# One kernel for a mixer, a mixture of experts and two gated layers: the first h tiles made in pairs, other counts of fillers, fewer transpositions ahead of the last sums

## The reference, cut to what matters

```python
mod = silu(c) @ w_mod + b_mod                       # 6 x 1024
sh1, sc1, gt1, sh2, sc2, gt2 = split(mod, 6)
h = rms_norm(x, g_norm1) * (1.0 + sc1) + sh1        # the opening
mix = hybrid_mixer(h, w_in, ...)                    # proj = h @ w_in and what follows
x = x + gt1 * mix
...                                                 # experts, then the second block
x = x + rms_norm(ffn2(rms_norm(x, g_pre)), g_post) * 0.5   # the end
```

## Time and profile before

| | |
|---|---|
| median of 3 runs | 2126.43 us (2124.46 to 2127.33) |
| profiled execution | 2119.8 us, its span 2117.8 us |
| PE busy | 2043.9 us, 97% of the span |
| DVE, ACT, POOL busy | 61%, 40%, 38% |
| mean granted TensorE clock | 0.980 |
| chain that ended last | PE 88%, DVE 6%, ACT 3% |

### The profile page before, as it was taken

How to read it: one execution, slowest core, us unless ns; L and a number is a source line. 1 busy time by engine, 2 the same in 40 slices (tenths; PEclk the granted TensorE clock), 3 DMA queues, 4 the chain that set the end, 5 groups by cost and what they waited for, 6 DMA issues and landing times.

```text
span 2117.8 us, 31232 instructions
## 1 busy us (share of the span) xinstructions
PE 2043.9 (97%) x12460; PEld 1745.8 (82%) x12460; DVE 1283.7 (61%) x1948; ACT 840.9 (40%) x1028; POOL 798.8 (38%) x605
## 2 busy tenths in 40 slices
PE   4999999999989999999999999999999998999998
PEld 4698787888767666679999999888878788999997
DVE  7375476665565666678677676331431359777775
ACT  7441355222354455544333333343332234333334
POOL 1342233544400000036666562221244545756661
PEclk7998999999999999999999999999999999999999
DMA  9121222555416999912322221211223212333321
GB/s 272 40 81 59 84 78 91 174 193 179 138 61 218 337 343 343 328 60 100 100 97 90 102 90 58 63 58 60 60 80 100 80 60 80 100 100 111 105 100 60
DMA packets 175763, 261.16 MB, mean 123 GB/s; under 512 B 12233, under 2 KB 140922, under 8 KB 175662
## 3 DMA queue, kind: packets, MB, share of 16 engines
q1 hardware_dynamic: 174126, 257.65, 36.4%
q10 hardware_dynamic: 1536, 2.10, 0.3%
HBM read 257.62 MB, written 2.11 MB: 123 GB/s over the span
## 4 chain that ended last, share of the span: by engine, by line
PE 88%; DVE 6%; ACT 3%; issue 1%; DMA 1%; SPq 0%; DVEq 0%; ACTq 0%
PE PS L829 65%; PE PS L1387 7%; PE PS L1427 4%; PE PS L1573 1%; PE PS L923 1%; ACT mod_early L1778 1%; PE PS L937 1%; DVE Hf L2428 1%; PE PS L1360 1%; PE PS L1442 1%; PE PS L1525 1%; DMA mod_early<-in_w_mod 1%; PE PS L1068 0%; PE PS L1028 0%; DMA w_raw<-in_w_ffn_in 0%
## 5 line engine op out<-in xcount | busy, mean ns | idle before, releaser
L740 POOL TENSOR_TENSOR w_lo<-w_raw,w_hi 128x512 fp32r<-128x512 f32 x444 | 596.0, 1373 | 1229.8 <-ACT w_hi L1756 871.1
L829 PE MATMUL PS<-HH,w_hi 128*128 128x512 f32 (+2 forms) x1408 | 469.1, 344 | 18.6 <-DVE HL L2351 4.6
L829 PE MATMUL PS<-HL,w_hi 128*128 128x512 f32 (+2 forms) x1408 | 464.7, 341 | 0.0
L829 PE MATMUL PS<-HH,w_lo 128*128 128x512 f32 (+2 forms) x1408 | 463.3, 340 | 0.0
L1756 ACT ACTIVATE w_hi<-w_raw 128x2048 fp32r<-128x2048 f32 x133 | 254.7, 1915 | 350.4 <-DVE w_raw L2389 124.8
L829 PEld LDWEIGHTS PS<-HH,w_hi 128*128 128x128 f32 x1408 | 262.1, 191 | 57.0 <-issue 15.2
L829 PEld LDWEIGHTS PS<-HH,w_lo 128*128 128x128 f32 x1408 | 262.1, 191 | 30.3
L829 PEld LDWEIGHTS PS<-HL,w_hi 128*128 128x128 f32 x1408 | 261.7, 190 | 29.3
L749 POOL TENSOR_TENSOR wx_lo<-wx_raw,wx_hi 128x512 fp32r<-128x512 f32 x132 | 187.7, 1450 | 0.0
L2926 DVE TENSOR_TENSOR m_lo<-m_raw,m_hi 128x2048 fp32r<-128x2048 f32 x56 | 128.3, 2292 | 70.0 <-ACT m_hi L2072 69.7
L3186 DVE TENSOR_TENSOR yacc<-yacc,PS 128x528 f32<-128x528 f32 (+1 forms) x176 | 117.9, 691 | 46.1 <-PE PS L829 44.7
(11 more groups left out here) (499 smaller groups left out, 4061.8 us busy)
## 6 DMA issues: line engine op xcount, KB each, us to landing
w_raw<-in_w_in SPq DMA_DIRECT2D x49, 1024.0 KB, 5.0
w_raw<-in_w_ffn_in SPq DMA_DIRECT2D x44, 1024.0 KB, 4.9
m_raw<-in_w_exp_gate SPq DMA_DIRECT2D x56, 512.0 KB, 4.0
m_raw<-in_w_exp_up SPq DMA_DIRECT2D x56, 512.0 KB, 5.2
m_raw<-in_w_exp_down SPq DMA_DIRECT2D x56, 512.0 KB, 4.7
w_raw<-in_w_ffn_out SPq DMA_DIRECT2D x22, 1024.0 KB, 4.8
mod_late<-in_w_mod SPq DMA_DIRECT2D x16, 1024.0 KB, 5.2
mod_early<-in_w_mod SPq DMA_DIRECT2D x8, 1024.0 KB, 11.9
```

The lines of the kernel that those rows point to most:

```text
L740: ins = pool.tensor_tensor(w_lo[:, s, cs], w_raw[:, s, cs], w_hi[:, s, cs].bitcast(F32), ALU.subtract)
L829: ins = mm(o, l, r, **k)
```

## The change

It touches four places.

1. **Loads.** SP loads w_mod tiles 0, 4, 1, 5, then the first w_in chunk, then tiles 2, 6, 3, 7.
2. **Opening.** Tiles 1, 2, 4 and 5 are multiplied by c on PE, tile 0 on DVE as before, and only 6, 3 and 7 go by ACT and DVE. They are worked through in the order 4, 0, 1, 5, 2, 6, 3, 7: PE does the first five ahead of the first chunk, 6 and 3 ahead of its k = 4, and 7 ahead of its k = 5. Gain, h, HH and HL are made for one pair of k at a time, on ACT with the scaling of 6, 3 and 7 between pairs 1 and 2. The results lie in the second bank of the slots, outside of the claims. ACT copies the second chunk's high part behind that of the small weights instead of ahead of it.
3. **Fillers.** hold goes from 8 to 11 in the norm behind the first mixer and in the one behind the first FFN, and in the norm behind the last mixer from 8 to 15, its idle from 28 to 14.
4. **End.** Only k = 0 to 3 are transposed ahead of the sums, for all four t; k = 4 to 7 behind them. The wait for the last released slots ahead of k = 4 goes.

```diff
...
-        MOD_PE = (1,)
-        MOD_SEQ = (1, 0, 2, 3, 4, 5, 6, 7)
+        MOD_PE = (1, 2, 4, 5)
+        MOD_SUMS = (0, 6, 3, 7)
+        MOD_SEQ = (4, 0, 1, 5, 2, 6, 3, 7)
+        MOD_LOADS = (0, 4, 1, 5), (2, 6, 3, 7)
...
-            for n in range(MOD1):
+            for n in MOD_LOADS[0]:
                 load_mod(n)
             cols("w_in", P1[0])
+            for n in MOD_LOADS[1]:
+                load_mod(n)
...
+            def early_mod(n):
+                at_ = MOD_SEQ.index(n)
+                if at_ >= SLOTS:
+                    pe.wait_ge(gain_ready, (at_ - SLOTS) // 2 + 1)
+                for m in range(2):
+                    o = PS[:, at_ % SLOTS, 1, m:m + 1]
+                    if n in MOD_PE:
+                        raw, landed, count = mod_slot(n)
+                        if m == 0:
+                            pe.wait_ge(landed, count)
                         for k in range(KT):
+                            ins = mm(o, raw[:, k, P * m:P * m + P], c_act[:, k:k + 1], start=k == 0, stop=k == KT - 1)
+                    else:
+                        d = mod_dve(n)
+                        if m == 0:
+                            pe.wait_ge(macc_ready, d + 1)
+                        ins = mm(o, macc[:, d % 2, P * m:P * m + P], ones[:, 0:1], start=True, stop=True)
+                ins.then_inc(mod_made, 1)
...
-            for n in MOD_SEQ:
-                mod_tile(n)
+            for n in MOD_SEQ[:5]:
+                early_mod(n)
...
             for k in range(KT):
+                if k == 4:
+                    early_mod(6)
+                    early_mod(3)
+                if k == 5:
+                    early_mod(7)
                 pe.wait_ge(hl_ready, hcount["hl"] + k + 1)
...
-            norm(SEQ, SQ_DENSE, 8, 5)
+            norm(SEQ, SQ_DENSE, 11, 5)
...
-            norm(TALL, SQ_DENSE, 8, 28)
+            norm(TALL, SQ_DENSE, 11, 28)
...
-            norm(SEQ, SQ_DENSE, 8, 28)
+            norm(SEQ, SQ_DENSE, 15, 14)
...
-            for k in range(KT - 1):
+            for k in range(4):
                 pe.wait_ge(yg_ready, k + 1)
-                if k == 4:
-                    for m in range(4, KT):
-                        W.wait_released(downs_at + m)
-                for t in range(NTOK - 1 if k >= 4 else NTOK):
+                for t in range(NTOK):
                     rows_of_y((s + 1 + t) % SLOTS, t, k)
...
-                for k in range(KT - 1 if t < NTOK - 1 else 4, KT):
+                for k in range(4, KT):
                     ins = rows_of_y(slot, t, k)
...
+            first_h(0)
             next_hi()
+            first_h(1)
+            scale_mod(6)
+            scale_mod(3)
+            scale_mod(7)
+            first_h(2)
+            first_h(3)
...
+            L(first_scaled(0, 2))
+            early_evac(4)
+            early_evac(0)
+            first_gain(0)
+            W.release(first_scaled(2, KT))
             W.wait_released(W.g - 1)
+            first_lo(0)
+            early_evac(1)
+            early_evac(5)
+            first_gain(1)
+            first_lo(1)
+            early_evac(2)
+            mod_sum(6)
+            mod_sum(3)
+            early_evac(6)
+            first_gain(2)
+            mod_sum(7)
+            early_evac(3)
+            first_lo(2)
+            early_evac(7)
+            first_gain(3)
+            first_lo(3)
```

More of the change, by code:

```diff
@@ L405, in build @@
         merged_tile = sem("merged_tile_final")
+        mod_made = sem("first_mod_products_made")
         yg_ready = sem("y_tile_times_gain")
@@ L541, in mod_dve @@
         def mod_dve(n):
-            return n - sum(m < n for m in MOD_PE)
+            return MOD_SUMS.index(n) if n < MOD1 else n - len(MOD_PE)
         def mod_slot(n):
@@ L963, in mod_tile @@
             def mod_tile(n):
[L964 to L968, removed]
-                        for k in range(KT):
[L970 to L979, removed]
+                d = mod_dve(n)
+                pe.wait_ge(macc_ready, d + 1)
+                s = W.claim()
+                for m in range(2):
+                    ins = mm(PS[:, s, 0, m:m + 1], macc_late[:, d % 2, P * m:P * m + P], ones[:, 0:1], start=True, stop=True)
+                W.made(ins)
+            def early_mod(n):
+                at_ = MOD_SEQ.index(n)
+                if at_ >= SLOTS:
+                    pe.wait_ge(gain_ready, (at_ - SLOTS) // 2 + 1)
+                for m in range(2):
+                    o = PS[:, at_ % SLOTS, 1, m:m + 1]
[3 more added lines that the diff above has]
+                            pe.wait_ge(landed, count)
+                        for k in range(KT):
+                            ins = mm(o, raw[:, k, P * m:P * m + P], c_act[:, k:k + 1], start=k == 0, stop=k == KT - 1)
+                    else:
+                        d = mod_dve(n)
+                        if m == 0:
+                            pe.wait_ge(macc_ready, d + 1)
+                        ins = mm(o, macc[:, d % 2, P * m:P * m + P], ones[:, 0:1], start=True, stop=True)
+                ins.then_inc(mod_made, 1)
             pe.wait_ge(consts, CONSTS)
@@ L1635, in _ @@
             swiglu(FF_UNITS, SEQ, rows_of_residual)
-            downs_at = W.g - KT
             s = W.claim()
             pe.wait_ge(rtok_ready, 2 * NTOK)
-            for k in range(KT - 1):
+            for k in range(4):
                 pe.wait_ge(yg_ready, k + 1)
-                if k == 4:
-                    for m in range(4, KT):
-                        W.wait_released(downs_at + m)
-                for t in range(NTOK - 1 if k >= 4 else NTOK):
+                for t in range(NTOK):
                     rows_of_y((s + 1 + t) % SLOTS, t, k)
@@ L1773, in _, with scale_mod @@
             act.wait_ge(cact_ready, 1)
-            for n in range(2, MOD1):
+            def scale_mod(n):
                 raw, landed, count = mod_slot(n)
@@ L1779, in _, with first_h @@
                 ins.then_inc(mod_scaled, 1)
-            next_hi()
[L1781 to L1790, removed]
+            def first_h(j):
+                act.wait_ge(gain_ready, j + 1)
+                for k in (2 * j, 2 * j + 1):
+                    h, gain, shift = Hf[:, k, 0:SEQ], gain1[:, k:k + 1], modc[:, k:k + 1]
+                    if k % 2:
+                        L(af(h, h, ACT.Identity, bias=shift, scale=gain))
+                        af(HH[:, k, 0:SEQ], h, ACT.Copy).then_inc(hh_ready, 1)
+                    else:
+                        af(HH[:, k, 0:SEQ], h, ACT.Identity, bias=shift, scale=gain).then_inc(hh_ready, 1)
+            first_h(0)
+            next_hi()
+            first_h(1)
[4 more added lines that the diff above has]
+            first_h(3)
+            W.skip(MOD_TILE)
             act.wait_ge(small_in, 16 * 10)
             af(w_small_hi[:, :, :], w_small[:, :, :], ACT.Copy).then_inc(small_hi, 1)
+            next_hi()
             def tm_tile(dst, c0, t):
@@ L2467, in mod_products @@
                     dve.sem_inc(mod_used, 1)
-            def mod_evac(n):
-                s = W.arrive()
-                W.release(tt(modc[:, 2 * n:2 * n + 2], PS[:, s, 0, 0:2], C1[:, 2 * n:2 * n + 2], ALU.add))
             for k in range(KT):
@@ L2491, in _, with first_scaled @@
             mod_products()
[L2492 to L2495, removed]
+            s_spread = W.arrive()
+            def first_scaled(k0, k1):
+                for k in range(k0, k1):
+                    ins = tt(Hf[:, k, 0:SEQ], R[:, k, META:TALL], ps(s_spread), ALU.mult)
+                return ins
             def mod_sum(n):
                 d = mod_dve(n)
-                dve.wait_ge(mod_scaled, n - 1)
+                dve.wait_ge(mod_scaled, d)
                 raw = mod_early[n]
@@ L2503, in mod_sum, with early_evac @@
                 tt(macc[:, d % 2, :], raw[:, 0, :], raw[:, 1, :], ALU.add).then_inc(macc_ready, 1)
[L2505 to L2511, removed]
-            W.wait_released(W.g - 1)
+            def early_evac(n):
+                at_ = MOD_SEQ.index(n)
+                dve.wait_ge(mod_made, at_ + 1)
+                L(tt(modc[:, 2 * n:2 * n + 2], PS[:, at_ % SLOTS, 1, 0:2], C1[:, 2 * n:2 * n + 2], ALU.add))
@@ new lines, in first_gain, with first_lo @@
+            def first_gain(j):
+                k, g = 2 * j, V1["g_norm1"] + 2 * j
+                L(stt(gain1[:, k:k + 2], modc[:, 8 + k:10 + k], 1.0, C1[:, g:g + 2], ALU.add, ALU.mult))
+                dve.sem_inc(gain_ready, 1)
+            def first_lo(j):
+                for k in (2 * j, 2 * j + 1):
+                    h = Hf[:, k, 0:SEQ]
+                    n_["hh"] += 1
+                    dve.wait_ge(hh_ready, n_["hh"])
+                    if k % 2 == 0:
+                        L(stt(h, h, gain1[:, k:k + 1], modc[:, k:k + 1].to_broadcast([P, SEQ]), ALU.mult, ALU.add))
+                    tt(HL[:, k, 0:SEQ], h, HH[:, k, 0:SEQ].bitcast(F32), ALU.subtract).then_inc(hl_ready, 1)
@@ L2514, in adaptive_gain, with mod_evac @@
+            first_lo(2)
```

(8 more changed lines are left out.)

## The result

The changed kernel takes 2129.82 us (median of 12 runs, 2120.80 to 2133.04), the kernel before 2124.35 us (12 runs, 2117.70 to 2127.33): ratio 1.0025, 95% interval 1.0014 to 1.0035. The change costs 5.5 us by the medians; the forecast was +2.4. The profiled execution has a span of 2127.7 us.

A forecast was written before the change was run, and what follows sets the result against it. PE was taken to set the time after ACT's scaling of w_mod tiles in the opening. Opening +4.3, last norm's fillers -1.4 and end -0.5 gave +2.4 us on 2126.4, thus 2128.8 us, range 2119 to 2133.

The forecast's parts named there:

- The passes at the low clock: Opening on PE: 96 passes for tiles 1, 5 and 2 run at 1.2 GHz, 0.213 us each, 20.4 us.
- Rival B: Opening on PE: one-column passes keep the high clock, small chunk at 53.5, total 2118 us; chance 0.17.
- The first product at 43.0: Opening on PE: the first w_in product starts at 43.0 us instead of 46.98.
- the lower bound: Opening: cost as low as 1.5 us if the clock falls later, each microsecond later saving 0.9, three allowed.
- The wait in front of k = 4: Opening: PE stands still 4.1 us before k = 4, waiting for DVE's work queued behind the copy of tile 6.
- The clock behind the gap: Opening: the clock falls in the gap before k = 4, so k = 4 takes 2.6 us, six products at 0.43.
- Rival A: PE between tile 3 and k = 4: clock returns only after k = 6 begins, about 4.5 us more, 2133; chance 0.17.
- The opening: Loads and w_mod tiles up to the small chunk: costs 4.3 us, between 1.5 and 7.
- The fillers of the last norm: Norm behind the last mixer: the 1.51 us gap closes and the clock holds, -1.4 us, bounds 0 to -1.6.
- The other two norms: Norms behind the first mixer and first FFN: six more passes fit the idle time, 0 us.
- The end: Last transpositions, sums and stores: sums start 1.0 us earlier, -0.5 us in all, between -0.2 and -1.0.
- C: Whole kernel: opening loses less and fillers win nothing, or the reverse; within 2 us of 2126; main case with it 0.66.

The follow-up runs named there:

- e3: Changed kernel with 128 equal moving columns instead of one in the early w_mod passes: 2118.67 us against 2122.28 for the kernel before, ratio 0.9988.
- e4: Changed kernel with four sum buffers, tile 7 summed on DVE ahead of the copy of tile 6: 2123.11 us against 2122.28 for the kernel before, ratio 1.0000.
- e1: Changed kernel's opening alone, with the fillers and end of the kernel before: 2129.82 us against 2122.28 for the kernel before, ratio 1.0033.
- e7: Kernel before with only the changed kernel's end (16 transpositions ahead of the last sums): 2121.62 us against 2121.92, ratio 0.9998.
- e2: Kernel before with the changed kernel's fillers and end, old opening kept: 2122.23 us against 2122.28, ratio 1.0004.
- e8: As e5, but 14 fillers behind the spread of the last post norm: 2113.68 us, ratio 0.9955 to the kernel before.
- e5: Changed kernel with 128-column passes, tiles 6 and 7 also on PE, 28 fillers behind the last norm's spread: 2110.93 us against 2121.92 for the kernel before, ratio 0.9950.
- e6: Kernel before with 15 instead of 8 fillers ahead of the last mixer's norm sums, 28 behind kept: 2122.14 us against 2121.92, ratio 1.0002.

## Why the prediction was right, and which of its terms were not

The time came out as forecast (2128.8, measured 2129.8), the direction too, but the change in time was half of the measured one: +2.4 for +5.5 us. That the time itself came within 1.0 us is partly luck. The forecast was built on the 2126.43 us of three runs, 2.1 us above the median of twelve (2124.35), and the change was put 3.1 us too low; the two errors nearly cancel. The largest chance stood on no difference that can be told, under 4.3 us, and the measured 5.5 lies just beyond that limit. By its steps:

*The passes at the low clock: right.* 96 x 0.213 = 20.4 us was the forecast, 20.62 is measured. Rival B (one-column passes keep the high clock) falls with the same row, and e3 shows why in one edit: the same number of passes on the same weights ran at a granted clock of 0.50 with one moving column and at 1.00 with 128. The rule of the Trainium skill ("TensorE: Matmul & The Clock Gate", Part 1), that activity releases the throttle, does not agree with this trace if the busy time of the profile is taken for activity: 20.40 us of unbroken busy time did not release it.

*The first product at 43.0: right* (43.40). The fall of the clock came 1.2 us earlier than in the kernel before (19.5 for 20.7), in the middle of tile 4, the reverse of what the lower bound had allowed for. It did no lasting harm: behind the first product the clock was back after 3.4 us (46.8), not after 4.4, and k = 0 to 3 ended at 50.59, where the forecast had 50.6.

*The wait in front of k = 4: right in place and cause, a little small.* Forecast 4.1 us, measured 4.57; DVE waits 0.58 us between the gain and the next sum, which had no place in the sum. e4 shows that the order on DVE makes the gap. *The clock behind the gap: right*, low up to 60.4. Rival A (low up to k = 6) did not come: the clock is back before k = 6 in the changed kernel (60.4 for 62.54), in e1 (60.8 for 62.45) and in e3 (53.3 for 54.30). It came close in e4, where k = 6 stands earlier (59.75) and the clock is back 0.4 us behind its first product.

*The opening: 4.3 forecast, 5.2 in the trace, 7.5 between the medians of e1 and its base.* Up to the gap PE was on the forecast's time. The 0.9 us come behind it: 0.5 at k = 4, which is the 0.58 us of waiting, 0.2 more up to the small chunk (65.42 for 64.7), and 0.15 because the kernel before began it at 60.25 and not at 60.4. Where the further 2 us in the medians come from was not settled; e1's interval (4.5 to 9.6 us) takes in the trace's number.

*The fillers of the last norm: -1.4 forecast, 0 measured. This is the term that was wrong.* The first half, that closing the gap holds the clock and wins 1.2 us, fits the profile of the kernel before and not every execution: in all seven profiles with 30 passes the clock stays up there, but with the old 16 it also stayed up in e7, so that in such an execution there is nothing to win. The step that failed is that the clock would stay up with half of the fillers behind the spread. The text had named it as a bound ("the thinner stretch after the 14") and priced it at the right size, but took the other value. The runs put in its place: with 14 the second norm loses 0.8 to 1.75 us against 26.24 in every profile (27.86, 27.99 and 27.87 us in the changed kernel, e2 and e8; 27.08 in e3 and e4), with 28 nothing is lost (26.24 in e5 and e6). What 15 and 28 win against 8 and 28 is 1.5 us in the executions that lose the clock behind the gap, and the medians of e6 cannot tell it from nothing. That PE's sums come later with 28 costs hardly anything, since DVE's clearing of yacc covers it, as the forecast had it: the spread begins 18.4 us behind the first filler in e5 and e6, and 18.3 in e3 and e4, where 14 fillers stand and the clock is high up to the spread.

*The other two norms: 0, right.* Their idle times were filled exactly, and there was no low clock to win back.

*The end: -0.5 forecast, -0.8 measured*, in the changed kernel and in e2, e5 and e7. Counted from the last product, DVE's rows start 0.8 us earlier and ACT's only 0.1; SP has issued its last store 0.5 us earlier. So ACT's start did not decide as much as taken. e7's interval holds both.

*C, the change does less than it says: no.* Its parts did what was asked of them.

Summed with the trace's terms: +5.2 + 0.1 - 0.8 = +4.5 us, for 5.5 between the medians with an interval of 3.0 to 7.4.

## What to carry to other kernels

A PE that the profile shows busy can still run at half its clock: before moving vector work onto PE as one-column products, look at the granted clock behind the ones that are there, and if it falls, give each pass more columns: 128 in place of one cost no time here and turned a loss of 5.5 us into a gain of 2.5 to 3.6. When work is moved into pairs, write down for each engine what stands behind the copy that it now waits for; one sum in the wrong place was half of this loss. A filler count is a trade of two stretches: fill the gap, and leave the stretch behind it as dense as it was. And before a gain is read from a pair of profiles, see whether another execution of the old code has it too.

## What the runs showed that was not expected

- A pass with 128 moving columns takes no longer than one with a single column at either clock: at 2.4 GHz 128 passes take 14.21 us in e5 from the first start to the product behind them (22.06 to 36.27), 0.111 us each, as one column in the earlier trace rows; at 1.2 GHz the eight passes of the spread take 1.70 us in the changed kernel (1752.88 to 1754.58), 0.213 each, as one column in the earlier trace rows. Only the wide ones kept the clock. That the weight load sets the distance of both is likely, since it is busy for 20.40 of 20.40 us in the opening, but no run isolates it.
- The scatter of one kernel's executions is of the size of the change: the kernel before took 2115.7 to 2128.5 us in 23 runs, and the profiled executions of two kernels with the same first 2100 us (before and e7) were up to 9.6 us apart: 3.1 us come in the first mixer (75 to 100 us), 1.4 in the experts, 4.2 in the first FFN; 1.5 are given back in the last norms, where e7 keeps the clock, and 2.8 come in the last FFN. At places where the code is the same, the clock stays low for longer in one of them. The first such place, in the kernel before and then in e7:

```profile
75.50:78.40 2.90, 2.90 (x14) 2.37 (x13) 0.00 (x0) 0.00 (x0) 0.04 (x1) 1.00 0.82 286
```

```profile
68.40:78.40 10.00, 9.90 (x22) 6.42 (x23) 4.45 (x6) 3.58 (x6) 4.97 (x4) 0.50 0.35 108
```

Before, the low stretch that begins at 68.5 us ends at 75.4; in e7 it ends at 78.5.
